# Two row passages of a three-layer kernel in another order

## The reference, cut to what matters

```python
def layer_norm(x, g, b):
    mu = jnp.mean(x, -1, keepdims=True)
    xc = x - mu
    var = jnp.mean(xc * xc, -1, keepdims=True)
    return xc * lax.rsqrt(var + LN_EPS) * g + b

# first passage: layer 0 -> projections of layer 1
x = layer_norm(DN_ALPHA * x + y, ln_g[0], ln_b[0])      # y = concat(...) @ w_out_even
h = x @ w_in_odd                                        # q, k, v, gate
# second passage: layer 1 -> projections of the second block
x = layer_norm(DN_ALPHA * x + y, ln_g[1], ln_b[1])      # y = (...) @ w_out_odd
hn = x * lax.rsqrt(jnp.mean(x * x, -1, keepdims=True) + 1e-5) * norm_mix_w
proj = hn @ w_in_2                                      # q, k, v, z, xbc, dt
```

## Time and profile before

| | before |
|---|---|
| median of 3 runs | 808.21 us (807.87 to 809.13) |
| the profiled execution | 807.91 us, span 806.1 |
| TensorE busy | 788.4 us, 98% |
| VectorE, ScalarE, GpSimd busy | 516.5 (64%), 411.8 (51%), 96.7 us (12%) |
| 16 load engines, mean busy | 53% |

### The profile page before, as it was taken

One profiled execution on the slowest core, in us unless ns is written; L12 is line 12 of the kernel. 1 busy time (PEld: TensorE's weight loads), 2 busy tenths in 40 slices (PEclk: granted clock), 3 DMA queues, 4 the chain that ended last, 5 costly groups with the idle time before them and its releaser, 6 DMA issues.

```text
span 806.1 us, 13073 instructions
## 1 busy us (share of the span) xinstructions
PE 788.4 (98%) x5082; PEld 693.3 (86%) x5082; DVE 516.5 (64%) x817; ACT 411.8 (51%) x613; POOL 96.7 (12%) x68
## 2 busy tenths in 40 slices
PE   9999999999999998999999899999999999999996
PEld 8998877799988886999787799899777999999995
DVE  6965557755655568467865874876756755555555
ACT  5534444453664443445764667466655544444441
POOL 2331000010100011111301207500000000000002
PEclk9999999999999999999999999999999999999999
DMA  9865644343864662675824364543317565656541
GB/s 330 314 195 178 202 157 137 97 152 106 245 212 137 190 209 77 207 221 176 255 85 135 105 209 133 183 143 120 104 54 220 186 227 179 207 169 199 176 138 52
DMA packets 76763, 137.43 MB, mean 170 GB/s; under 512 B 7072, under 2 KB 15520, under 8 KB 76704
## 3 DMA queue, kind: packets, MB, share of 16 engines
q1 hardware_dynamic: 75456, 132.15, 51.2%
q0 software_dynamic: 1248, 4.46, 1.7%
HBM read 132.80 MB, written 1.05 MB: 166 GB/s over the span
## 4 chain that ended last, share of the span: by engine, by line
PE 90%; DVE 5%; issue 2%; ACT 1%; POOL 1%; POOLq 0%; DVEq 0%; ACTq 0%
PE acc L1035 13%; PE acc L1043 13%; PE acc L1037 13%; PE acc L1036 13%; PE acc L1045 12%; PE acc L1044 12%; PE acc L1314 1%; PE acc L1348 1%; DVE w_lo L777 1%; PE acc L1191 1%; PE acc L1298 1%; PE acc L1287 1%; PE acc L1227 1%; PE acc L1183 1%; POOL v_lo L2352 1%
## 5 line engine op out<-in xcount | busy, mean ns | idle before, releaser
L777 DVE TENSOR_TENSOR w_lo<-raw,w_hi 128x1024 fp32r<-128x1024 f32 (+1 forms) x224 | 273.0, 1234 | 184.0 <-ACT w_hi L757 95.9
L1043 PE MATMUL acc<-x_hi,w_hi 128*128 128x256 f32 x840 | 240.2, 286 | 0.4 <-DVE x_lo L2135 0.4
L1045 PE MATMUL acc<-x_hi,w_lo 128*128 128x256 f32 x840 | 237.6, 283 | 0.0
L1044 PE MATMUL acc<-x_lo,w_hi 128*128 128x256 f32 x840 | 237.6, 283 | 0.0
L757 ACT ACTIVATE w_hi<-raw 128x1024 fp32r<-128x1024 f32 (+1 forms) x128 | 133.4, 1044 | 141.7 <-PE acc L1045 71.7
L747 ACT ACTIVATE w_hi<-raw 128x1024 fp32r<-128x1024 f32 x109 | 116.0, 1064 | 116.1 <-PE acc L1045 63.0
L1043 PEld LDWEIGHTS acc<-x_hi,w_hi 128*128 128x128 f32 x840 | 160.7, 191 | 3.2 <-issue 2.5
L1044 PEld LDWEIGHTS acc<-x_lo,w_hi 128*128 128x128 f32 x840 | 160.8, 191 | 0.9 <-issue 0.5
L1045 PEld LDWEIGHTS acc<-x_hi,w_lo 128*128 128x128 f32 x840 | 160.7, 191 | 0.0
L1035 PE MATMUL acc<-w_hi,cat_hi 128*128 128x512 f32 x272 | 109.0, 401 | 0.2 <-DVE w_lo L777 0.2
L1037 PE MATMUL acc<-w_hi,cat_lo 128*128 128x512 f32 x272 | 106.9, 393 | 0.0
(11 more groups left out here) (286 smaller groups left out, 914.3 us busy)
## 6 DMA issues: line engine op xcount, KB each, us to landing
raw<-in_w_ff SPq DMA_DIRECT2D x32, 1024.0 KB, 5.2
raw<-in_w_in_even SPq DMA_DIRECT2D x28, 1024.0 KB, 5.1
raw<-in_w_in_odd SPq DMA_DIRECT2D x16, 1024.0 KB, 5.6
raw<-in_w_in SPq DMA_DIRECT2D x16, 1024.0 KB, 5.6
raw<-in_w_out_even SPq DMA_DIRECT2D x12, 1024.0 KB, 5.1
raw<-in_w_out SPq DMA_DIRECT2D x4, 1024.0 KB, 5.0
raw<-in_w_in_even SPq DMA_DIRECT2D x4, 512.0 KB, 6.4
raw<-in_w_ukv_even SPq DMA_DIRECT2D x8, 256.0 KB, 3.2
```

Source lines behind the costliest of these rows:

```text
L777: ins = eng.tensor_tensor(lo, r, hi.bitcast(F32), ALU.subtract)
L1043: pe.matmul(o, wh[:, k, fs], hi[:, ka, :], start=start and f % 2 == 0, stop=False, skip_group_check=True)
L1044: pe.matmul(o, wh[:, k, fs], lo[:, ka, :], start=False, stop=False, skip_group_check=True)
L1045: ins = pe.matmul(o, wl[:, k, fs], hi[:, ka, :], start=False, stop=stop, skip_group_check=True)
```

## The change

First passage: centring is done by halves, each followed by its normalisation; `turn_rows` is split by halves, with a product step between; `x_lo` of the second half comes after a statistics row. VectorE makes only the first half of `first`'s low part; GpSimd makes its second half (share `REST`) and, after the rows of t = 0 are normalised, both halves of `second`'s. Second passage: `v` is loaded ahead of the two last `w_out_odd` pieces, and the raw slots follow the loading order; its parts are made in three steps (`wide_first`, `wide_hi`, `wide_lo`), the low part by VectorE. Squares come before dt's and conv's high parts on ScalarE; the fillers `BUSY_SPLIT` are removed; the transposes of t = 1 come before dt's products of t = 0; `x_lo` of t = 0 is made in two pieces around the normalisation of t = 1.

```diff
-BUSY_SPLIT = (3, 2)
-WIDE = 8
+REST = 3
@@ plan
-    for s in (("tokens", (last_two[1], 1, 0, 3)), ("turn_rows", 0), ("tokens", (last_two[1], 1, 3, 4)),
-              ("part", (first, 0, 0, 4)), ("part", (second, 0, 0, 3)), ("turn_rows", 1), ("part", (second, 0, 3, 4)),
+    for s in (("tokens", (last_two[1], 1, 0, 3)), ("turn_rows", (0, 0)), ("tokens", (last_two[1], 1, 3, 4)), ("turn_rows", (0, 1)),
+              ("part", (first, 0, 0, 4)), ("part", (second, 0, 0, 3)), ("turn_rows", (1, 0)), ("part", (second, 0, 3, 4)), ("turn_rows", (1, 1)),
               ("part", (first, 1, 0, 4)), ("part", (second, 1, 0, 4)), v_end):
...
+        rows_pieces["v"].ahead_of = rows_pieces["out"][0]
...
-    between[16].append(last_pieces)
+    between[16] += [last_pieces, lambda: step("wide_first", rows_pieces["v"])]
     between[17] = [lambda: first_of_last("sides", 2)]
+    between[18] = [lambda: step("wide_hi", rows_pieces["v"])]
     between[19] = [lambda: first_of_last("out", 1)]
     pipeline(8, MOBA_HEADS, 2, between)
-    step("wide_weights", rows_pieces["v"])
+    step("wide_lo", rows_pieces["v"])
...
-    for t in range(T):
-        step("mix_turn", t)
-        step("rows_of", (rows_pieces["v"], t, 0, 8))
-        if t:
-            step("epi", rows_pieces["v"].chunk)
-        step("rows_of", (rows_pieces["dt"], t, 0, 8))
+    step("mix_turn", 0)
+    step("rows_of", (rows_pieces["v"], 0, 0, 8))
+    step("mix_turn", 1)
+    step("rows_of", (rows_pieces["dt"], 0, 0, 8))
+    step("rows_of", (rows_pieces["v"], 1, 0, 8))
+    step("epi", rows_pieces["v"].chunk)
+    step("rows_of", (rows_pieces["dt"], 1, 0, 8))
@@ pool_share
             if p in by_rows:
-                return 2 * by_rows.index(p)
+                return (REST, 4)[by_rows.index(p)]
@@ TensorE, mix_turn
-                keep_busy(acc[:, v_piece.chunk.pair, 1, :], BUSY_SPLIT[t])
@@ ScalarE
                 elif kind == "mix_rows":
+                    row_squares(0)
                     hi_prep(act, own, dt_piece.n)
-                    hi_first(act, own, conv_piece.n)
-                    row_squares(0)
+                    row_scaled(0)
                 elif kind == "mix_turn":
                     row_hi(i)
                     if i == 0:
+                        hi_first(act, own, conv_piece.n)
+                        row_squares(1)
+                        row_scaled(1)
+                    else:
                         hi_rest(act, own, conv_piece.n)
-                        row_squares(1)
-                    else:
                         hi_first(act, own, conv_piece.n + 1)
@@ VectorE, first_norm
-                own(dve.scalar_tensor_tensor(tmp[:, t * D:(t + 1) * D], res[:, t, :], stats[:, 32 + 2 * t:33 + 2 * t], R2[:, 0:D], ALU.subtract, ALU.mult))
-                own.wait()
-                dve.wait_ge(*due("rows_rstd", t + 1))
                 for h in range(2):
...
+                    own(dve.scalar_tensor_tensor(tmp[:, o:o + NCOL], res[:, t, hs], stats[:, 32 + 2 * t:33 + 2 * t], R2[:, hs], ALU.subtract, ALU.mult))
+                    own.wait()
+                    if h == 0:
+                        dve.wait_ge(*due("rows_rstd", t + 1))
@@ VectorE, first_rows
-                    rows_lo(0)
+                    rows_lo(0, 0)
                     row_part(0, 1)
+                    rows_lo(0, 1)
@@ VectorE, new steps
+                elif kind == "wide_first":
...
+                    (r, hi, lo), = split_views(i, 0, 4)
+                    own(dve.tensor_tensor(lo, r, hi.bitcast(F32), ALU.subtract))
+                elif kind == "wide_lo":
+                    dve.wait_ge(*due("hi_ready", i.n + 1))
+                    (r, hi, lo), = split_views(i, 4, 8)
+                    own(dve.tensor_tensor(lo, r, hi.bitcast(F32), ALU.subtract), "lo_ready")
@@ VectorE, mix_rows
+                    row_mean_square(0)
                     row_part(0, 1)
-                    row_mean_square(0)
...
-                    row_lo(0)
+                    row_lo(0, 0, 2)
                     row_normed(1)
+                    row_lo(0, 2, 4)
+                    row_mean_square(1)
                     low_prep(dt_piece.n)
-                    row_mean_square(1)
-                    row_lo(1)
+                    row_lo(1, 0, 4)
@@ GpSimd
                 elif kind == "weights":
-                    room_free(pool, i)
-                    low_prep(i.n)
+                    if i is by_rows[0]:
+                        room_free(pool, i)
+                        low_prep(i.n)
                 elif kind == "first_rows":
...
+                        if t == 0:
+                            pool.wait_ge(*due("rows_done", 1))
+                            room_free(pool, by_rows[1])
+                            low_prep(by_rows[1].n)
```

More of the change, by code:

```diff
@@ L713, in build @@
         for p in pieces:
-            count += p.full and pool_share(p) < 2
+            count += p.full and pool_share(p) in (0, 1, REST)
             n_first[p.n] = count
@@ L784, in build @@
         loads = [0] * RAW_SLOTS
+        loading = [p for p in pieces if not p.ahead_of]
         for p in pieces:
+            if p.ahead_of:
+                loading.insert(loading.index(p.ahead_of), p)
+        for at, p in enumerate(loading):
+            p.slot = at % RAW_SLOTS
+            p.slot_before = loading[at - RAW_SLOTS] if at >= RAW_SLOTS else None
             srcs = p.src if isinstance(p.src, list) else [p.src]
@@ L1140, in part, with turn_rows @@
                 products_of_tokens(p, t, k0, k1)
-            def turn_rows(t):
-                pe.wait_ge(*due("rows_half", t + 1))
-                for k in range(KD):
-                    if k == 4:
-                        pe.wait_ge(*due("rows_done", t + 1))
-                    ins = pe.transpose(aux[:, 2 * t + k // 4, (k % 4) * P:(k % 4 + 1) * P], res[:, t, k * P:(k + 1) * P], ident)
-                    if k % 4 == 3:
-                        own(ins, "rows_turned")
-                if t:
+            def turn_rows(t, h):
+                pe.wait_ge(*due("rows_done" if h else "rows_half", t + 1))
+                for k in range(4 * h, 4 * h + 4):
+                    ins = pe.transpose(aux[:, 2 * t + h, (k % 4) * P:(k % 4 + 1) * P], res[:, t, k * P:(k + 1) * P], ident)
+                own(ins, "rows_turned")
+                if t and h:
                     state["x"] += 1
@@ L1805, in row_mean_square, with row_lo @@
                     "mix_mean")
-            def row_lo(t):
-                for b in range(4):
+            def row_lo(t, b0, b1):
+                for b in range(b0, b1):
                     dve.wait_ge(*due("mix_hi", 4 * t + b + 1))
```

105 lines of the change are left out of this document (52 added, 53 removed).

## The result

The changed kernel took 802.54 us (median of 4 runs, 801.62 to 803.53), the kernel before 808.67 (807.87 to 809.35) beside it: ratio 0.9919, 95% interval 0.9905 to 0.9933, 6.1 us faster. Run again beside later experiments it took 802.64 (801.99 to 804.04) against 809.07: ratio 0.9923 (0.9911 to 0.9936). The forecast was 803.1 in a range of 801.6 to 805.4, made from a kernel before at 808.21; as a gain it was 5.1 us. The profiled execution took 803.11 us with a span of 801.3; before it was 807.91 and 806.1.

A forecast was written before the change was run, and what follows sets the result against it. TensorE, busy 98% of the span, was taken as the bound, with its waits and low clock to be won. Gains of 4.1 + 1.0 = 5.1 us gave 802.8 on the profile's clock, 803.1 beside the median; range 801.6 to 805.4.

The forecast's parts named there:

- The start of the row work: First passage: VectorE's second addition for t = 0 starts 3.6 us earlier, removing TensorE's whole 3.29 us wait and low clock.
- The new idles of the first passage: First passage: TensorE newly idles 0.25 us for `x_lo`, then 0.6 and 0.15 for the normalised halves of t = 1.
- The price of the low clock: First passage: nine matmuls at half clock after the 3.29 us wait cost a further 1.7 us, which the change wins back.
- The rival that would have made it slower: First passage: GpSimd's `b_lo` holds all VectorE work, TensorE idles 4.9 us, the clock falls again; 808.7 us, chance 0.03.
- Nor was VectorE late: Rival, first passage: VectorE remains late, halves of t = 1 come 1 to 2 us later; 805.0 us, chance 0.11.
- The two-SBUF centring of t = 1: First passage: only the first centring half of t = 1, due at 307.5, waits for `b_lo` on GpSimd until 307.9.
- The second passage: From v's load to the first convolution product: earlier centring, squares and transposes bring that product from 464.33 to 463.35, gain 1.0 us.
- The fifth `x_lo`: Second passage, v's products of t = 0: it is ready at 454.9, TensorE wants it at 453.95, so 1.0 us idle.
- The clock rival: Second passage: without fillers, TensorE's idles let the clock fall, losing 1.0 us; 804.1 us, chance 0.22.

The follow-up runs named there:

- the shares alone: Kernel before, with `v_lo`'s second half and both halves of `b_lo` on GpSimd, centring and transposes left whole: 804.95 us, ratio 0.9946.

## Why the prediction was right

**The start of the row work.** Forecast: VectorE 3.6 us sooner, the whole 3.29 us of idle gone and the low clock with it. Measured: VectorE 3.69 sooner, idle 3.29 to 0, clock 1.00 throughout. That it is the move of the low parts which does it is shown by the shares alone (4.08 of 4.33); the halves bring 0.25 by themselves and 0.25 on top of the shares.

**The new idles of the first passage.** Forecast 0.25 + 0.6 + 0.15; measured 0.44 (half of it behind `x_lo`) + 0.17. Two terms off, in opposite directions; the sum of 1.0 was 0.6.

**The price of the low clock.** Forecast 1.7, from the length of the low stretch alone. In the order of before the clock was worth 0.58, by two kernels: the one with the wait filled, and the one without GpSimd's half of `b_lo` (1.66 less 1.08). In the changed kernel it is worth more: A lost 3.06 us of idle on balance (3.29 + 0.38 less 0.44 + 0.17) and 4.33 in all, which leaves 1.27 for the clock less the added switches between transposes and products (0.2 in the forecast). The term came near there only because t = 1's rows had become early as well, a condition that the prediction did not state.

**The rival that would have made it slower** (GpSimd's `b_lo` holds all of VectorE) had its answer in the addition of 0.68 beside `b_lo`; it didn't happen. Nor was VectorE late. The two-SBUF centring of t = 1 met the end of `b_lo`, as forecast, for 0.34 (0.4 forecast).

**The second passage.** Forecast 1.0, measured 1.41 in the changed kernel and 1.07 with this passage alone. The fifth `x_lo` was waited for 0.69, not 1.0, which the transposes of t = 1 then had: 1.70 sooner in place of 1.4. v's early low part is worth 1.03 at the first transposes, the cut of the `x_lo` 0.87 at C, and the two fillers 0.85 at C. These don't add to 1.41, since each is measured with the others in place. That the whole came out near the forecast is in part luck: the time was 0.6 us off and the gain 1.0, both passages gave more than forecast (0.2 and 0.4 by the marks), and the terms inside them were off in both directions.

**The clock rival.** I gave 0.22 to a fall of the clock in the second passage, at a price of 1.0. The first profile had none; the second had one, at 0.17. So the mechanism exists, and in that one trace its price was well under the one set, since a slowed TensorE waits less for `x_lo`. For the order of before, 1.0 is right (0.92 and 1.06 at C, in two traces). What the fall depends on is open: the kernel before waited 2.05 us in the second passage without one, with only the first passage edited the same wait was followed by a fall in two kernels and by none in three. The Trainium skill ("TensorE: Matmul & The Clock Gate", part 1) ties the fall to an idle period, and by that the shorter gaps of the new order should have been safe; the trace of the repeated kernel, with a fall in a gap of 1.76, doesn't agree.

**The medians moved by 6.1 and 6.4 us,** the marks by 4.33 + 1.41 = 5.7. That lies inside both intervals (5.4 to 7.7 and 5.2 to 7.2), so there may be nothing to explain. One reading, if there is: the kernel before has more executions with a second fall than its profile shows. Of its 60 timed runs beside the experiments 27 have a mean granted clock of 0.994 or less, with a mean time of 809.6, the other 33 a mean of 808.4; the profile shown is of the latter kind, and none of the changed kernel's 9 runs is of the former. This is argued from the clocks and not shown in a trace, since the mean clock also holds the idle tail of the span.

## What to carry to other kernels

Ask first whether two engines can run side by side on the same kind of operand: half of `b_lo` on the slower engine made VectorE later than all of it on the faster one, and what helped was to give GpSimd its share at a time at which VectorE reads PSUM. Don't add the low clock's price to a wait's without asking when the engines behind are ready: it was worth 0.6 us where their next work was late, and some 1.3 where that had become early too. A filler is free only inside a wait: three cost nothing, and two, a few microseconds on, 0.85.

## What was unexpected of the hardware

The same wait of 3.29 us was followed by a low clock of 3.4 us in one execution and of 5.6 us and more in another, which set in before the wait had ended. A wait of 2.21 us in the first passage was followed by none. The 2.05 us of the second passage were followed by none in four profiles and by a low clock in two, and one of 1.76 by a low clock of about 3.5 us that began inside it (the repeated kernel) or not at all (the first profile of it). Low stretches in the second passage were seen in five of the 13 profiles taken beside that of the kernel before; each followed waits of 1.1 us or more, as there are in seven of the other eight too; the one without (fillers put back, longest wait 0.69) kept its clock. So one profile doesn't tell what a gap costs; a term for the clock needs a chance beside its price.
